# Making the low halves of six weight strips on GpSimd in a hybrid encoder block

## The chip, the cores and the metric

The kernel runs on one core of a Trainium2 chip. The metric is the device time of one execution in microseconds, the median over repeated runs. One execution was also profiled; every row below comes from that one.

## The reference

One encoder block on x of 512 tokens by 1024 channels, all in float32:

```
h = rms_norm(x);  z = h @ w_in                      # one combined projection
qa, ka, va, qb, kb, vb, ga, gb = split(z)
ya = axial_gqa_attention(qa, ka, va) @ w_o_a        # mixer A: 8 query heads on 2 key heads
yb = dilated_window_attention(qb, kb, vb) @ w_o_b   # mixer B: 12 heads in 3 dilation groups
x = x + (sigmoid(ga + ba) * ya + sigmoid(gb + bb) * yb) @ w_out
x = x + expert_choice_swiglu(rms_norm(x))           # 16 experts, 64 tokens each
y = rms_norm(x)
```

## The kernel before

Large matmuls are done in a rounded format on two parts of each operand, a high and a low half, and as three products (high by high, high by low, low by high). The weights of the projections come as *strips* of 128 columns: 128 partitions by 1024 float32, numbered in the order of use. A strip goes through four hands. SP loads it into a raw buffer (`w_raw`, a ring of four homes, L577 to L599; a load waits until the strip that had the home before is split). ScalarE copies it into `w_hi`, which rounds it (`split_hi`, L794 to L805, semaphore `w_hi_done`). VectorE subtracts, `w_lo = w_raw - w_hi` (`split_lo`, L1888 to L1892, semaphore `w_split`). TensorE waits for `w_split` before its first matmul with the strip (`wait_split`, L540).

Strips 0 to 11 make mixer A's q, k, v and mixer B's v. Strips 12 to 17 are the first q and k strips of mixer B, strips 18 and 19 the first two of its second half. All four engines have an order written out by hand.

Mixer A works on 32 tiles u (8 heads by 4 query tiles of 128). For each tile TensorE makes the scores (`scores_a`, L1326, two tiles ahead), VectorE takes the row maximum from PSUM (L2015), ScalarE the exponentials with their sum (L889), VectorE the reciprocal (L1985) and the product with it, the normalisation (L1987, `probs_normed`), TensorE turns the tile by transposes (`turn_probs`, L1357), ScalarE copies it out of PSUM (L901), and after each eight tiles TensorE multiplies by the values (`values_a`, L1369). Between the scores and the transposes of a tile TensorE does one to three steps of mixer B's q and k projection (`fill`, `col_steps`, L1169 to L1171). These steps read strips 12 to 18; the results are split too (L920 and L2003 for q, L923, L924, L2007 and L2008 for k).

VectorE's loop over the tiles places the low halves of strips 14 to 19 by the list `A_LOWS`:

```
if u in A_LOWS:                       # A_LOWS = (5, 7, 10, 16, 20, 26)
    split_lo(14 + A_LOWS.index(u))
```

Behind the loop VectorE waits for the distance table, copies a part of it (L2033) and goes on to mixer B, whose tiles it serves with L2052, L2058 and again L1985 and L1987. The later low halves (strip 20 on) stay with VectorE.

GpSimd has short work: the reciprocal square roots of the norms (`power`, L716 to L719, a TENSOR_SCALAR and a TENSOR_TENSOR with a power), the last ones for mixer A in the stretch from 50 to 63 us, then nothing until the second norm at 378 us, where it also makes three 128x512 subtractions (L755).

Of the kernel before, what the change touches and what calls it, by code (L numbers as in the profile page):

```python
# [84 lines left out]
def encoder_block(nc, x, norm1_g, w_in, b_gates, q_norm_g, k_norm_g, w_o_a, w_o_b, w_out, norm2_g,  # L85
# [139 lines left out]
    with ExitStack() as ctx:  # L225
# [250 lines left out]
        A_LEAD = 6  # L476
        A_FILL = [min(N_COL_A * KC, A_LEAD + 2 + (i + 1) * (N_COL_A * KC - A_LEAD - 2) // (NA - 1)) for i in range(NA)]
        O_READ, O_LOW = (10, 19, 26), (11, 21, NA)
        A_LOWS = (5, 7, 10, 16, 20, 26)
        B_HIGHS, B_LOWS = (NA + 4, NA + 6, NA + 7), (NA + 6, NA + 7, NA + 8)  # L480
        B_FILL = ([2, 3, 4, 5, 7, 8, 8, 8], [3, 6, 7, 8, 11, 14, 16, 16])

# [219 lines left out]
        @block.gpsimd  # L702
        def _(pool):
            pool.memset(neg_half, -0.5).then_inc(neg_half_set, 1)
            pool.memset(aff_wide[:, :, NE:2 * NE], 0.0).then_inc(masks_set, 1)
            pool.wait_ge(neg_half_set, 1)

            steps = [0]

            def settle(ins):  # L710

                ins.then_inc(pool_step, 1)
                steps[0] += 1
                pool.wait_ge(pool_step, steps[0])

            def power(sums, into, n, width, done):  # L716

                settle(pool.tensor_scalar(into, sums, 1.0 / width, EPS, ALU.mult, ALU.add))
                pool.tensor_tensor(into, into, neg_half[:, 0:n], ALU.pow).then_inc(done, 1)  # L719

            def power_of_sum(c):

                pool.wait_ge(ssq3, c + 1)
                settle(pool.tensor_scalar(rstd[:, c:c + 1], ssq[:, c:c + 1], 1.0, EPS, ALU.mult, ALU.add))
                pool.tensor_tensor(rstd[:, c:c + 1], rstd[:, c:c + 1], neg_half[:, 0:1], ALU.pow).then_inc(rstd3, 1)

            def rstd_of_x(c):
                pool.wait_ge(sumsq_done, c + 1)
                power(ssq[:, c:c + 1], rstd[:, c:c + 1], 1, D, rstd_done)

            for c in range(NT):
                rstd_of_x(c)

            w = A_HEADS + A_KV
            for c in range(NT):
                pool.wait_ge(a_sumsq, c + 1)
                power(ssqA[:, w * c:w * c + w], rstdA[:, w * c:w * c + w], w, HD, a_rstd)

            for c in range(NT):
                pool.wait_ge(sumsq2, c + 1)  # L740
                if c == NT - 1:
                    pool.wait_ge(sumsq2, NT + 1)
                    settle(pool.tensor_tensor(ssq[:, c:c + 1], ssq[:, c:c + 1], ssq_half[:, 0:1], ALU.add))
                power(ssq[:, c:c + 1], rstd[:, c:c + 1], 1, D, rstd2)
            pool.wait_ge(logits_done, NT)
            pool.memset(all_rows[:, :].bitcast(F32), 1.0).then_inc(masks_set, 1)
            pool.memset(later[:, 0:1].bitcast(F32), 0.0).then_inc(masks_set, 1)
            pool.memset(same_row[:, :, :, 0], 0.0).then_inc(masks_set, 1)
            pool.memset(same_row[:, :, :, 1:NT], 1.0).then_inc(masks_set, 1)
            pool.iota(row_steps[:, :], [[1, NT]], base=0, channel_multiplier=NT).then_inc(masks_set, 1)  # L750
            pool.wait_ge(aff_done, NT)
            for n, (c, h) in enumerate(LOW_BY_POOL):
                pool.wait_ge(xn_hi_done, c + 1)
                cols = slice(SEQ * h, SEQ * h + SEQ)
                pool.tensor_tensor(xn_lo[:, c, cols].rearrange("p (k i) -> p k i", k=HALF),  # L755
                                   x2[:, c, cols].rearrange("p (i k) -> p k i", k=HALF),
                                   xn_hi[:, c, cols].rearrange("p (k i) -> p k i", k=HALF).bitcast(F32),
                                   ALU.subtract).then_inc(xn_lo_pool, 1)
            pool.wait_ge(aff_lo_done, 1)
            pool.memset(ones_row[0:1, :], 1.0).then_inc(ones_row_set, 1)  # L760
            for c in range(NT):
                power_of_sum(c)
            pool.wait_ge(row_ms, 1)
            pool.tensor_tensor(ssq_half[:, 2:3], ssq_half[:, 2:3], neg_half[:, 0:1], ALU.pow).then_inc(rstd3, 1)
            pool.wait_ge(out_written, 16)
            pool.wait_ge(give_done, PAIRS)
            pool.wait_ge(fin_act_done, 1)
            pool.wait_ge(fin_done, NT + 1)
            pool.indirect_dma_start(out[0], bass.IndirectOffsetOnAxis(row_at[:, 0:1], 0), rows[:, :], None,
                                    bounds_check=SEQ - 1, oob_is_err=False).then_inc(rows_written, 16)  # L770
# [1089 lines left out]
        def _(dve):  # L1860
# [27 lines left out]
            def split_lo(n):  # L1888

                dve.wait_ge(w_hi_done, n + 1)  # L1890
                raw, hi, lo = parts_of(n)
                dve.tensor_tensor(lo, raw, hi.bitcast(F32), ALU.subtract).then_inc(w_split, 1)  # L1892
# [119 lines left out]
            for u in range(NA + 5):  # L2012
                if u < NA:
                    dve.wait_ge(score_done, u + 1)
                    dve.tensor_reduce(column(nmax, u), pp[u % 3][:, :], AX, ALU.max, negate=True)\  # L2015
                        .then_inc(nmax_done, 1)
                if 1 <= u <= NA:
                    norm_probs(u - 1, SEQ)
                for g in range(N_COL_A):
                    filled = filled_at(A_FILL, g)  # L2020
                    if u == (filled + 3 if g < N_COL_A - 1 else NA + 2):
                        low_col(g, 0)
                    if u == (filled + (6 if g == N_COL_A - 3 else 4) if g < N_COL_A - 1 else NA + 3):
                        low_col(g, 1)
                if u == 2:
                    low_k(1)
                if u in A_LOWS:
                    split_lo(14 + A_LOWS.index(u))
                if u in O_LOW:
                    low_o(O_LOW.index(u))  # L2030

            dve.wait_ge(dist_in, 16)
            settle(dve.tensor_copy(far[:, :], dist[:, 0, SEQ:SEQ + 2 * P]))  # L2033
            for hp in range(2):
                first, end = NA + 2 * NT * hp, NA + 2 * NT * (hp + 1)
                if hp:
                    for g in range(2 * NG + 2, 4 * NG):
                        low_col(g, 0)
                        low_col(g, 1)
                        split_lo(at[col_groups[g][1:]] + RING)  # L2040
                for u in range(first, end + 2):
                    if u == first + 1:
                        if hp == 0:
                            norm_probs(first, SEQ + 2 * P)
                        low_o(OA - 1 + hp)
                    if u < end:
                        head, c = divmod(u - NA, NT)

                        dve.wait_ge(score_done, NA + 2 * (u - NA) + 1)
                        dve.tensor_tensor(dist[:, c, SEQ:SEQ + 2 * P],  # L2052
                                          far_two[u % 2][:, 1, :, :].rearrange("p g n -> p (g n)"), far[:, :],
                                          ALU.add).then_inc(far_added, 1)
                        dve.wait_ge(far_added, u - NA + 1)
                        dve.wait_ge(score_done, NA + 2 * (u - NA) + 2)
                        wait_probs_free(dve, u)
                        dve.tensor_tensor_reduce(probs_of(u)[:, :], scores_two[u % 2], dist[:, c, :],  # L2058
                                                 -SLOPES[head], HUGE, ALU.add, ALU.min,
                                                 column(nmax, u)).then_inc(nmax_done, 1)  # L2060
                    if first + 1 - hp < u <= end:
                        norm_probs(u - 1, SEQ + 2 * P)
                    if hp == 0:
                        filled = first + filled_at(B_FILL[0], 0)
                        if u == filled + 3:
                            low_col(N_COL_A, 0)
                            low_col(N_COL_A, 1)
                        if u in B_LOWS:
                            split_lo(at[col_groups[2 * KC // RING + B_LOWS.index(u)][1:]] + RING)
                        if u == filled + 4:  # L2070
                            split_lo(at[col_groups[N_COL_A][1:]] + RING)
                    for g in range(2) if hp else ():
                        if u == first + filled_at(B_FILL[1], g) + 2:
                            split_lo(at[("ga", 0)] + g + RING)
# [378 lines left out]
```

## Time and profile before

| what | value |
|---|---|
| time, median of 3 runs | 862.43 us (862.28 to 864.42) |
| the profiled execution | 861.86 us |
| its span, first to last instruction | 859.8 us |
| granted TensorE clock, mean | 0.998 |
| TensorE busy | 839.4 us, 98% |
| VectorE busy | 379.3 us, 44% |
| ScalarE busy | 264.1 us, 31% |
| GpSimd busy | 29.0 us, 3% |
| HBM read | 235.92 MB |

Busy shares are means over stages with different limits; mixer A is the stretch from about 87 to 162 us, mixer B from there to about 245 us, the gates and the output projection to about 390 us, and the experts the rest. PE is TensorE's matmul side, PEld its weight loads, DVE is VectorE, ACT ScalarE, POOL GpSimd. In timelines the first number is the start and the second the duration, both in us.

### The profile page before, as it was taken

The page shows a single profiled execution, that of the slowest core. Times are in us where ns is not written, and L with a number is a line of the kernel's source. Part 1 is how long each engine was busy: PE and PEld are TensorE (multiplying, and loading weights), DVE is VectorE, ACT ScalarE, POOL GpSimd, SP SyncE. Part 2 cuts the span into 40 slices and gives each one's busy share as a digit, 9 for nine tenths or more (in the row PEclk, how much of TensorE's full clock was granted, in tenths as well). Part 3 has the DMA queues.
Part 4 walks back from the last instruction along what each step waited for, and adds up shares of the span by engine and source line. Part 5 has one row for each costly group of instructions (what it writes and reads, how often), then busy time and mean ns, then how long its engine had stood idle before and what let it go on. Part 6 is the DMA issues. An engine that isn't in the chain of part 4 may idle for free.

```text
span 859.8 us, 10399 instructions
## 1 busy us (share of the span) xinstructions
PE 839.4 (98%) x4197; PEld 513.2 (60%) x4197; DVE 379.3 (44%) x665; ACT 264.1 (31%) x461; POOL 29.0 (3%) x50
## 2 busy tenths in 40 slices
PE   9999999999999999999999999999999998989996
PEld 8898866687878888888534343344433433334343
DVE  6377987797715254427322237223131321321351
ACT  6333876695624233216011010010100101001231
POOL 1050000000000000003000000000000000000010
PEclk9999999999999999999999999999999999999999
DMA  9830112023034234884899999999999999999996
GB/s 285 179 98 2 50 50 98 25 76 109 20 123 143 84 107 144 311 356 180 331 410 425 429 428 426 429 428 427 428 428 427 426 430 428 426 423 429 427 420 265
DMA packets 81490, 239.19 MB, mean 278 GB/s; under 512 B 8102, under 2 KB 63526, under 8 KB 65828
## 3 DMA queue, kind: packets, MB, share of 16 engines
q1 hardware_dynamic: 76016, 235.94, 69.7%
q10 hardware_dynamic: 5284, 2.09, 1.0%
q8 instruction: 33, 0.54, 0.3%
q0 software_dynamic: 144, 0.51, 0.1%
q14 instruction: 13, 0.11, 0.0%
HBM read 235.92 MB, written 2.62 MB: 277 GB/s over the span
## 4 chain that ended last, share of the span: by engine, by line
PE 88%; DMA 8%; DVE 1%; ACT 1%; issue 1%; POOLq 0%; POOL 0%; SPq 0%; DVEq 0%; ACTq 0%
PE psum L1657 21%; PE psum L1169 11%; PE psum L1689 11%; PE psum L1171 11%; PE psum L1170 11%; DMA wslot<-in_w_down 7%; PE psum L1614 3%; PE psum L1708 3%; PE psum L1357 2%; PE psum L1818 2%; PE psum L1326 2%; PE psum L1369 1%; PE psum L1669 1%; PE psum L1175 1%; PE psum L1622 1%; PE psum L1379 1%
## 5 line engine op out<-in xcount | busy, mean ns | idle before, releaser
L1657 PE MATMUL psum<-wslot,xinT 128*64 128x512 f32 x1000 | 221.9, 595 | 3.7 <-DMA wslot<-in_w_up 1.9
L1657 PEld LDWEIGHTS psum<-wslot,xinT 128*64 128x64 f32 x1000 | 69.5, 137 | 141.3 <-issue 131.8
L1689 PE MATMUL psum<-wslot,actT 128*64 128x512 f32 x424 | 95.8, 596 | 4.5 <-DMA wslot<-in_w_down 4.5
L1169 PE MATMUL psum<-hT_hi,w_hi 128*128 128x512 f32 x208 | 82.4, 396 | 0.9 <-DVE oT_lo L1991 0.9
L1170 PE MATMUL psum<-hT_lo,w_hi 128*128 128x512 f32 x208 | 81.2, 390 | 0.0
L1171 PE MATMUL psum<-hT_hi,w_lo 128*128 128x512 f32 x208 | 81.2, 390 | 0.0
L1892 DVE TENSOR_TENSOR w_lo<-w_raw,w_hi 128x1024 fp32r<-128x1024 f32 (+1 forms) x46 | 52.9, 1174 | 44.4 <-ACT w_hi L805 44.3
L1689 PEld LDWEIGHTS psum<-wslot,actT 128*64 128x64 f32 x424 | 29.4, 137 | 60.4 <-issue 58.0
L1101 ACT ACTIVATE actT<-psum 128x512 f32<-128x512 f32 x16 | 9.6, 597 | 171.2 <-PE psum L1669 171.2
L2305 DVE TENSOR_TENSOR x<-x,psum 128x512 f32<-128x512 f32 x48 | 29.7, 681 | 57.0 <-PE psum L1708 57.0
L2295 DVE TENSOR_TENSOR y_lo<-psum,y_hi 64x512 fp32r<-64x512 f32 x28 | 19.3, 689 | 80.4 <-ACT y_hi L1111 80.0
L805 ACT ACTIVATE w_hi<-w_raw 128x1024 fp32r<-128x1024 f32 (+1 forms) x46 | 45.2, 1017 | 16.3 <-PE psum L1171 16.3
L1169 PEld LDWEIGHTS psum<-hT_hi,w_hi 128*128 128x128 f32 x208 | 39.0, 188 | 12.1 <-issue 2.8
L1171 PEld LDWEIGHTS psum<-hT_hi,w_lo 128*128 128x128 f32 x208 | 39.1, 188 | 8.4
L1170 PEld LDWEIGHTS psum<-hT_lo,w_hi 128*128 128x128 f32 x208 | 39.1, 188 | 7.8
L1096 ACT ACTIVATE act<-psum,slot_vals 128x512 f32<-128x512 f32 x16 | 11.0, 687 | 93.2 <-PE psum L1657 93.2
L2282 DVE SCALAR_TENSOR_TENSOR act<-psum,slot_vals,act 128x512 f32<-128x512 f32 x16 | 12.0, 750 | 59.1 <-ACT act L1096 59.0
L901 ACT ACTIVATE pT<-psum 128x512 f32<-128x512 f32 x48 | 28.5, 596 | 19.6 <-PE psum L1357 10.1
L1111 ACT ACTIVATE y_hi<-psum 64x512 fp32r<-64x512 f32 x28 | 16.5, 590 | 57.3 <-PE psum L1689 57.0
L1614 PE MATMUL psum<-xn,pick 128*128 128x512 f32 x120 | 29.4, 396 | 0.0
L2248 DVE TENSOR_TENSOR xinT<-psum,small 128x512 f32<-128x512 f32 x15 | 9.7, 686 | 40.0 <-PE psum L1622 40.0
L2288 DVE SCALAR_TENSOR_TENSOR act<-act,slot_fac,psum 128x512 f32<-128x512 f32 x16 | 12.0, 747 | 30.8 <-PE psum L1657 30.8
(285 smaller groups left out, 1306.5 us busy)
## 6 DMA issues: line engine op xcount, KB each, us to landing
wslot<-in_w_up SPq DMA_DIRECT2D x24, 2048.0 KB, 25.0
wslot<-in_w_gate SPq DMA_DIRECT2D x24, 2048.0 KB, 23.9
wslot<-in_w_down SPq DMA_DIRECT2D x22, 2048.0 KB, 22.4
w_raw<-in_w_in SPq DMA_DIRECT2D x34, 512.0 KB, 4.7
wslot<-in_w_up SPq DMA_DIRECT2D x15, 1024.0 KB, 11.0
wslot<-in_w_down SPq DMA_DIRECT2D x15, 1024.0 KB, 27.5
wslot<-in_w_gate SPq DMA_DIRECT2D x14, 1024.0 KB, 11.2
w_raw<-in_w_out SPq DMA_DIRECT2D x8, 512.0 KB, 4.9
```

The source lines that it names most:

```text
L805: act_.activation(hi, raw, ACT.Copy).then_inc(w_hi_done, 1)
L901: last = act_.activation(pT[:, head % 2, :, cols], tp[(0, 3)[u % 2]][:, :].rearrange("p (k i) -> p k i", i=P), ACT.Copy)
L1169: pe.matmul(out_, s_hi, m_hi, start=(k == 0), stop=False)
L1170: pe.matmul(out_, s_hi, m_lo, start=False, stop=False)
L1171: return pe.matmul(out_, s_lo, m_hi, start=False, stop=(k == n_k - 1))
L1614: mm = pe.matmul(bank[6 + f][:, :], pick[:, c, :, :], part[:, c, cols], start=(c == 0 and part is xn_hi), stop=(c == NT - 1 and part is xn ...
L1657: mm = pe.matmul(bank[2 * e + n][CAP * f:CAP * f + CAP, :], xinT[:, HALF * h + k, CAP * e:CAP * e + CAP], wslot[place_of(m)][:, k % PART, ...
L1689: mm = pe.matmul(bank[4 + e][CAP * f:CAP * f + CAP, :], actT[:, e, k, CAP * h:CAP * h + CAP], wslot[place_of(m)][:, k % PART, SEQ * f:SEQ ...
L1708: mm = pe.matmul(bank[added_bank(c, f)][:, :], give[:, p % 2, P * c:P * c + P], part[:, SEQ * f:SEQ * f + SEQ], start=(part is y_hi), stop ...
L1892: dve.tensor_tensor(lo, raw, hi.bitcast(F32), ALU.subtract).then_inc(w_split, 1)
L2295: dve.tensor_tensor(y_lo[rows, cols], bank[4 + e][CAP * f:CAP * f + CAP, :], y_hi[rows, cols].bitcast(F32), ALU.subtract).then_inc(y_lo_do ...
L2305: dve.tensor_tensor(part, part, bank[added_bank(c, f)][:, :], ALU.add).then_inc(added, 1)
```

## The change

The low halves of strips 14 to 19 are taken out of VectorE's loop and put into GpSimd's list, behind the reciprocal square roots of mixer A. GpSimd waits for the split before (`w_split` counts strips in order) and for the high half, and makes the same subtraction. VectorE waits, ahead of mixer B, until the last of the six is done, so that the count stays in order.

```
-        A_LOWS = (5, 7, 10, 16, 20, 26)
+        POOL_SPLITS = range(14, 20)
...
+            for n in POOL_SPLITS:
+                pool.wait_ge(w_split, n)
+                pool.wait_ge(w_hi_done, n + 1)
+                raw, hi, lo = parts_of(n)
+                pool.tensor_tensor(lo, raw, hi.bitcast(F32), ALU.subtract).then_inc(w_split, 1)
...
-                if u in A_LOWS:
-                    split_lo(14 + A_LOWS.index(u))
                 if u in O_LOW:
                     low_o(O_LOW.index(u))
 
             dve.wait_ge(dist_in, 16)
             settle(dve.tensor_copy(far[:, :], dist[:, 0, SEQ:SEQ + 2 * P]))
+            wait_split(dve, POOL_SPLITS[-1])
```

## Rows read from the trace of the kernel before

**Rows 1.** The page: busy time by engine; DMA share in 40 slices, in tenths.

```profile
PE 839.4 (98%) x4197; PEld 513.2 (60%) x4197; DVE 379.3 (44%) x665; ACT 264.1 (31%) x461; POOL 29.0 (3%) x50
...
DMA  9830112023034234884899999999999999999996
```

**Rows 2.** Windows: stretch, length, busy PE, PEld, DVE, ACT, POOL, clock, DMA share, GB/s.

```profile
75.00:100.00 25.00, 25.00 (x128) 20.62 (x127) 19.48 (x38) 17.02 (x33) 0.00 (x0) 1.00 0.00 1
...
120.00:140.00 20.00, 19.98 (x104) 14.05 (x103) 15.40 (x32) 14.06 (x30) 0.00 (x0) 1.00 0.18 51
...
405.00:860.00 455.00, 438.37 (x2068) 188.68 (x2066) 135.32 (x242) 59.39 (x98) 6.76 (x13) 1.00 0.98 414
```

**Rows 3.** Waits of TensorE's weight loads, 83 to 163 us: total, times, longest.

```profile
PEld psum L1357 <- DVE probs_a L1987: 2.1, 7, 0.5
```

**Rows 4.** Groups by form, VectorE: busy us, mean ns, idle before.

```profile
L1892 DVE TENSOR_TENSOR w_lo<-w_raw,w_hi 128x1024 fp32r<-128x1024 f32 x38 | 45.8, 1220 | 44.0 <-ACT w_hi L805 43.9
...
L1987 DVE TENSOR_SCALAR probs_a<-probs_a,small 128x512 f32<-128x512 f32 x32 | 15.6, 487 | 1.1
...
L1987 DVE TENSOR_SCALAR probs_b<-probs_b,small 128x768 f32<-128x768 f32 x16 | 9.9, 620 | 0.6
...
L1892 DVE TENSOR_TENSOR w_lo<-w_raw,w_hi 128x768 fp32r<-128x768 f32 x8 | 7.6, 952 | 0.4 <-ACT w_hi L805 0.4
```

**Rows 5.** Groups by form, the nearest subtractions and products of GpSimd and VectorE.

```profile
L755 POOL TENSOR_TENSOR xn<-x,xn 128x512 fp32r<-128x512 f32 x3 | 4.5, 1535 | 0.8 <-DVE aff_wide L2140 0.8
...
L718 POOL TENSOR_SCALAR small<-small 128x1 f32<-128x1 f32 x8 | 1.5, 192 | 338.2 <-ACT squares L1016 327.0 <-ACT squares L783 11.1
...
L2148 DVE TENSOR_TENSOR xn<-x,xn 128x512 fp32r<-128x512 f32 x5 | 5.4, 1092 | 1.9 <-ACT xn L1044 1.9
...
L1957 DVE TENSOR_TENSOR zA<-zA,small 128x640 f32<-128x640 f32 x4 | 3.3, 821 | 0.1
```

**Rows 6.** Timelines of GpSimd and VectorE, 50 to 62 us.

```profile
50.30 1.11 POOL L718 TENSOR_SCALAR small<-small 128x10 f32<-128x10 f32 x1 [34.95 <-DVE small L1951]
...
54.39 0.89 POOL L718 TENSOR_SCALAR small<-small 128x10 f32<-128x10 f32 x1
55.37 2.80 POOL L719 TENSOR_TENSOR small<-small 128x10 f32<-128x10 f32 x1
...
61.00 0.32 POOL L718 TENSOR_SCALAR small<-small 128x10 f32<-128x10 f32 x1
...
50.13 2.35 DVE L1892 TENSOR_TENSOR w_lo<-w_raw,w_hi 128x1024 fp32r<-128x1024 f32 x2
...
54.00 2.35 DVE L1892 TENSOR_TENSOR w_lo<-w_raw,w_hi 128x1024 fp32r<-128x1024 f32 x2
```

**Rows 7.** Timelines of ScalarE, VectorE and TensorE, 92 to 101 us.

```profile
92.69 1.05 ACT L805 ACTIVATE w_hi<-w_raw 128x1024 fp32r<-128x1024 f32 x1
...
93.86 0.49 DVE L1987 TENSOR_SCALAR probs_a<-probs_a,small 128x512 f32<-128x512 f32 x1
...
98.45 1.22 DVE L1892 TENSOR_TENSOR w_lo<-w_raw,w_hi 128x1024 fp32r<-128x1024 f32 x1
...
94.47 0.59 PEld L1357 LDWEIGHTS psum<-ident,probs_a 128*128 128x128 f32 x4
...
100.24 0.40 PE L1169 MATMUL psum<-hT_hi,w_hi 128*128 128x512 f32 x1
```

**Rows 8.** Timelines of the same engines, 119 to 125 us.

```profile
119.95 1.05 ACT L805 ACTIVATE w_hi<-w_raw 128x1024 fp32r<-128x1024 f32 x1
...
122.25 0.49 DVE L1987 TENSOR_SCALAR probs_a<-probs_a,small 128x512 f32<-128x512 f32 x1
...
124.02 0.59 PEld L1357 LDWEIGHTS psum<-ident,probs_a 128*128 128x128 f32 x4
```

**Rows 9.** Timelines of ScalarE and VectorE, 134 to 136 us.

```profile
134.22 1.06 ACT L805 ACTIVATE w_hi<-w_raw 128x1024 fp32r<-128x1024 f32 x1
...
135.43 0.49 DVE L1987 TENSOR_SCALAR probs_a<-probs_a,small 128x512 f32<-128x512 f32 x1
```

## The prediction

> **What bounds the kernel now.** I read the page first, then windows by stage, the waits, the groups of lines, and last the timelines of the instants at which the moved work runs. The page shows TensorE busy for 98% of the span, VectorE for 44%, GpSimd for 3%, and DMA near full only from the 21st slice of 40 on [rows 1]. The windows say which stage has which limit: from 75 to 162 us (mixer A) TensorE has no gap worth naming, at a granted clock of 1.00 (the 2.4 GHz level), while VectorE is busy over three quarters of the time and GpSimd does nothing; from 405 us the expert weights stream at 414 GB/s [rows 2]. TensorE's order is fixed, and the expert stream starts only when the stages before it have let go of SBUF, so a microsecond that TensorE loses in mixer A should reach the end of the kernel whole, and one gained too.
>
> VectorE is nearly a second bound there. The only VectorE wait that TensorE's weight loads show in mixer A is for normalised probabilities: 2.1 us in 7 waits, the longest 0.5 [rows 3]; the matmuls in flight cover it, for no matmul waits in that stretch. So 2.1 us is a ceiling on what a faster VectorE can return in this stage.
>
> **The change part by part.** *Removed from VectorE:* six subtractions of 1.22 us, 7.3 us in all [rows 4]. The trace has them at 98.45, 101.97, 108.47, 122.66, 135.83 and 148.51 us (the first stands in [rows 7]). Each sits right behind a normalisation and delays the next. Some of the seven waits come from this, others sit where no subtraction is; I take 0.3 us as the gain, between 0 and 2.1.
>
> *Added to GpSimd:* six subtractions 128x1024. The trace has none. The nearest row is its 128x512 subtraction, 1.535 us, which reads with a step; VectorE takes 1.092 us for that same stepped shape, yet 0.821 us for a plain 128x640 with two SBUF inputs [rows 5], which at 1.05 ns an element [rows 4] is 0.69 for a plain 512: a ratio of 1.6. Twice 1.535 less one fixed part of about 0.2 (a one-element GpSimd TENSOR_SCALAR takes 0.192 [rows 5]) gives 2.9 us as the upper end; dividing the per-element part, 2.7, by VectorE's 1.6 gives 1.9 as the lower end. I take 2.3, about the middle, since nothing says whether the step costs GpSimd as much as VectorE. The page GPSIMD Engine Reference (section 3) of the Trainium skill has 4.5 us for 2048 elements, which by halving would be an estimate of about 2.3 too.
>
> *When they run.* GpSimd now starts as soon as ScalarE has the high half, not where VectorE's list put it: the high halves, six rows of L805 of which the second, fifth and sixth stand in [rows 7, 8, 9], end at 91.17, 93.74, 98.02, 108.05, 121.00 and 135.28 us. With 2.3 us each, all low halves are ready earlier than now: the first by 94 us, where TensorE first reads that strip at 100.24 us and VectorE now finishes it only at 99.67 [rows 7]. Even 2.9 us each keeps 5 us of margin, and the later strips have more. So TensorE never waits for a strip. SP, which waits for a split before it refills that buffer, issues its loads of the next strips earlier; the DMA share of this stretch is 0.18 or less [rows 2], and ScalarE's place for the next high half is set by its list, so this costs and gives nothing. The new wait of VectorE on the sixth low half stands ahead of mixer B at 165.7 us, 25 us after GpSimd is done; behind it are the first scores of mixer B, but it costs at most a few hundredths. After 63.4 us GpSimd has nothing until 378 us, so nothing else queues behind the six.
>
> *The port.* This is where the change can hurt. GpSimd's four TENSOR_SCALARs of ten elements are the same work, yet took 1.11 us at 50.30, 0.89 at 54.39 and 0.32 at 61.00. The first ended at 51.41, just past the end at 51.35 of the VectorE subtraction started at 50.13; the second at 55.28, past the end at 55.22 of the one started at 54.00 [rows 6]. So GpSimd waits for a whole VectorE instruction with two SBUF inputs: something is exclusive between the two engines. What the trace doesn't show is the reverse, a long GpSimd read in front of VectorE. The VectorE instruction at risk in mixer A is the normalisation L1987: 0.487 us for 512 elements and 0.620 for 768, that is 0.52 ns an element where the subtraction with two inputs needs 1.05 (1.220 against 0.952 us for 1024 and 768) [rows 4]. It moves two elements at a time. The other VectorE instructions of the stage read PSUM and at most one SBUF tensor. I take it that what holds one way holds the other: a GpSimd subtraction reading 1024 elements of two tensors keeps L1987 out from its start to its end.
>
> The page SBUF — State Buffer (section "Who interferes with whom") of the Trainium skill says the shared pair is an exclusive lock, kept for the full instruction by whichever engine came first, with the other wholly blocked, and names tensor_scalar in its two-port mode among those that take it. By that rule the sum below holds; if only VectorE can hold GpSimd up, rival (a) does. The trace, 51.41 behind 51.35 us, agrees in one direction; no row of it has the other.
>
> *The cost, if GpSimd blocks the normalisation.* Due times are the L1987 starts, need times the L1357 loads of the same tile.
> Strips one to three: the first subtraction runs 91.46 to 93.76 (it waits for the normalisation that began at 90.97) and hits nothing. The second starts at about 93.82, just ahead of the normalisation due at 93.86 [rows 7], which then ends at 96.12 + 0.49 = 96.61 where TensorE wanted it at 94.47: 2.15 lost. The third falls, everything being shifted, beside the normalisation due at 98.05 or the next: between 0.45 and 2.3 more; I take 0.5.
> Strip four, at 108 us, lies under the attention values (normalisations are 3.8 us early there): 0.
> Strip five: 121.44 to 123.74; the normalisation due at 122.25 ends at 124.23, wanted at 124.02 [rows 8]: 0.2.
> Strip six: ready to start at 135.28 + 0.08, and the normalisation is due at 135.43 [rows 9]; if GpSimd is first it ends at 137.66 + 0.49 = 138.15 instead of 135.92: 2.2.
> Sum 2.15 + 0.5 + 0.2 + 2.2 = 5.1, less 0.3 gained: 4.8 us. Lost TensorE time isn't given back, because behind it TensorE is again the bound.
>
> The profiled execution took 861.86 us (span 859.8 and 2.1 around it), so it would come to 866.7; it stands 0.6 under the median of the runs, 862.43, and against that median the forecast is 867.2 us.
>
> **The rivals.** What this kernel's measurement can tell from no change is about 0.3%, 2.6 us.
> (a) *GpSimd doesn't hold VectorE up*, or does so piece by piece. For: the GpSimd power at 55.37, 2.80 us long, left VectorE's list without a gap [rows 6]; against: it reads ten elements. Then only the 0.3 gain and the wait remain: 862.1 to 862.9, the same. This is the outcome on the other side; it decides if L1987 stays at 0.49 us during GpSimd's subtractions.
> (b) *It blocks, but the near ties fall VectorE's way.* At 93.82 against 93.86 and 135.36 against 135.43 there are under 0.1 us between the two. If VectorE comes first both times, GpSimd starts 0.5 later and hits only the following normalisation: about 0.4 each. With 0.45 and 0.2 the sum is 1.5, less 0.3: 863.6, the same within what can be told.
> (c) *All ties fall GpSimd's way and an operation is 2.9 us:* 2.8 + 2.3 + 1.4 + 2.8 = 9.3, less 0.3: 871.4.
> (d) *VectorE's relief is worth more than the waits show.* To be faster by 2.6 us it would have to return more than the whole 2.1 of waits. A gain of that kind would need the relief to reach mixer B, where VectorE waits for ScalarE anyway: 859.5.
> (e) *GpSimd becomes late with a strip.* It needs an operation above 6 us, twice the upper bound; under 2%.
>
> **How the numbers follow.** Blocking with a loss above 2.6 us (the forecast, and (c) as its tail) 0.53; (b) 0.15; (a) 0.28; (d) 0.04. Slower by over 0.3%: 0.53; within: 0.43; faster: 0.04. The likeliest case alone spans 865.0 to 871.4. The range for 8 in 10 has to take in (a), so it goes from 861.9 to 870.3, and leaves out (d) and most of (c).
>
> **What would show it.** Six TENSOR_TENSOR rows on GpSimd between 91 and 138 us, of 1.9 to 2.9 us; L1987 with a few instances of 2 us or more, or late starts behind them, at the second and the sixth; the waits of L1357 for L1987 rising from 2.1 us to about 7; mixer B's first score matmul starting about 4.8 us later, and the distances unchanged from there. If L1987 keeps a maximum of 0.5 us, the port step is wrong and (a) holds. If GpSimd's rows are longer than 2.9 us because VectorE interrupts them, the lock isn't held for the whole instruction. If the loss sits behind 165 us instead, the added wait did it and my reading of the order is wrong.

## The result, and the profile after

| | before | after |
|---|---|---|
| median | 863.13 us | 868.59 us |
| lowest to highest, 10 runs each | 861.93 to 865.23 | 865.83 to 871.63 |
| ratio, 95% interval | | 1.0064 (1.0050 to 1.0079) |
| profiled execution | 861.86 us | 868.40 us |
| its span | 859.8 us | 866.6 us |
| granted TensorE clock, mean | 0.998 | 0.993 |

The change makes the kernel slower by 0.64%. The forecast was 867.2 us against 862.43, a ratio of 1.0055. Four executions of the experiments below took far longer than all others of their version (e1 once 1430.6 us, e2 955.6 and 4871.8, e4 955.77); they are counted in the medians given there, not in the ratios.

The page of the changed kernel, busy time by engine, answers to [rows 1]. Line numbers behind L743 are 4 to 6 higher than before: L1987 is now L1993, L1357 is L1363, L805 is L811.

```profile
PE 842.4 (97%) x4197; PEld 515.6 (60%) x4197; DVE 381.0 (44%) x659; ACT 264.4 (31%) x461; POOL 43.6 (5%) x56
```

GpSimd gained 14.6 us. VectorE lost six subtractions of 1.22 us, 7.3 us, and yet is busy 1.7 us longer, not shorter. The groups by form show where the time went; columns as in [rows 4]:

```profile
L743 POOL TENSOR_TENSOR w_lo<-w_raw,w_hi 128x1024 fp32r<-128x1024 f32 x6 | 14.6, 2440 | 62.1 <-ACT w_hi L811 62.1
...
L1898 DVE TENSOR_TENSOR w_lo<-w_raw,w_hi 128x1024 fp32r<-128x1024 f32 x32 | 38.5, 1220 | 44.0 <-ACT w_hi L811 43.9
L1993 DVE TENSOR_SCALAR probs_a<-probs_a,small 128x512 f32<-128x512 f32 x32 | 23.6, 738 | 1.1
```

The 32 normalisations of mixer A went from 487 ns on average [rows 4] to 738: 8.0 us more for the same work. (8.0 less 7.3 is 0.7 of VectorE's 1.7; the page counts time in which any instruction runs, the groups add up instructions, which overlap at their ends.) The timelines of GpSimd and VectorE (start, duration) show that few of them carry all of it:

```profile
94.07 2.36 POOL L743 TENSOR_TENSOR w_lo<-w_raw,w_hi 128x1024 fp32r<-128x1024 f32 x1 [0.15 <-ACT w_hi L811]
100.53 2.62 POOL L743 TENSOR_TENSOR w_lo<-w_raw,w_hi 128x1024 fp32r<-128x1024 f32 x1 [4.10 <-ACT w_hi L811]
109.94 2.36 POOL L743 TENSOR_TENSOR w_lo<-w_raw,w_hi 128x1024 fp32r<-128x1024 f32 x1 [6.80 <-ACT w_hi L811]
123.67 2.54 POOL L743 TENSOR_TENSOR w_lo<-w_raw,w_hi 128x1024 fp32r<-128x1024 f32 x1 [11.37 <-ACT w_hi L811]
137.95 2.35 POOL L743 TENSOR_TENSOR w_lo<-w_raw,w_hi 128x1024 fp32r<-128x1024 f32 x1 [11.75 <-ACT w_hi L811]
...
91.17 0.48 DVE L1993 TENSOR_SCALAR probs_a<-probs_a,small 128x512 f32<-128x512 f32 x1
...
94.05 2.66 DVE L1993 TENSOR_SCALAR probs_a<-probs_a,small 128x512 f32<-128x512 f32 x1
...
100.40 0.49 DVE L1993 TENSOR_SCALAR probs_a<-probs_a,small 128x512 f32<-128x512 f32 x1
...
101.59 1.83 DVE L1993 TENSOR_SCALAR probs_a<-probs_a,small 128x512 f32<-128x512 f32 x1
...
110.93 1.66 DVE L1993 TENSOR_SCALAR probs_a<-probs_a,small 128x512 f32<-128x512 f32 x1
...
123.47 0.49 DVE L1993 TENSOR_SCALAR probs_a<-probs_a,small 128x512 f32<-128x512 f32 x1
...
124.78 1.71 DVE L1993 TENSOR_SCALAR probs_a<-probs_a,small 128x512 f32<-128x512 f32 x1
...
137.96 2.63 DVE L1993 TENSOR_SCALAR probs_a<-probs_a,small 128x512 f32<-128x512 f32 x1
```

Add start and duration: the stretched normalisation of 94.05 ends at 96.71, where GpSimd's operation ends at 96.43; the others end 0.27 to 0.29 us behind theirs in the same way (103.42 and 103.15, 112.59 and 112.30, 126.49 and 126.21, 140.59 and 140.30). VectorE holds GpSimd up too: the two operations that began just behind the start of a normalisation (100.53 behind 100.40, 123.67 behind 123.47) took 2.62 and 2.54 us instead of 2.36.

What reached TensorE: the waits from 83 to 168 us (the weight loads' answer to [rows 3]; then the matmuls', of which before had none), and the two matmuls that waited.

```profile
PEld psum L1363 <- DVE probs_a L1993: 6.1, 5, 2.6
...
PE psum L1363 <- DVE probs_a L1993: 3.9, 2, 2.2
```
```profile
96.77 0.44 PE L1363 MATMUL psum<-ident,probs_a 128*128 128x128 f32 x2 [1.73 <-DVE probs_a L1993]
...
140.65 0.66 PE L1363 MATMUL psum<-ident,probs_a 128*128 128x128 f32 x4 [2.17 <-DVE probs_a L1993]
141.06 0.98 PE L1332 MATMUL psum<-kA,qA 128*128 128x512 f32 x2
141.83 0.63 PE L1175 MATMUL psum<-hT_hi,w_hi 128*128 128x512 f32 x1
...
143.97 0.63 PE L1177 MATMUL psum<-hT_hi,w_lo 128*128 128x512 f32 x1
...
145.46 0.39 PE L1175 MATMUL psum<-hT_hi,w_hi 128*128 128x512 f32 x1
```

Two gaps, each behind one of the two longest normalisations. Behind the second the projection matmuls take 0.63 us instead of 0.39 for some 3.4 us. The windows say why; the eighth column is the granted clock:

```profile
75.00:100.00 25.00, 23.27 (x118) 19.05 (x117) 19.54 (x34) 15.50 (x30) 4.77 (x2) 1.00 0.15 43
...
140.00:145.00 5.00, 4.36 (x17) 3.53 (x18) 3.50 (x8) 2.04 (x5) 0.31 (x1) 0.66 0.36 105
145.00:150.00 5.00, 5.00 (x28) 4.16 (x27) 4.22 (x9) 4.64 (x9) 0.00 (x0) 1.00 0.02 4
```

Full clock, 2.4 GHz, around the first gap and again from 145 us; a mean of 0.66 between 140 and 145, that is the 1.2 GHz level for about two thirds of it, after an idle stretch of 2.17 us. The start of each matmul, compared with the start of the same matmul before, gives the account: 0.2 us were there at 80 us already (the clock was low from 8 to 12 us too, a mean of 0.57 where before has 1.00), 1.9 come at the first gap, 0.3 and 0.2 at the next two tiles' transposes, 2.1 at the last gap, 1.5 in the slow stretch. Mixer B's first score matmul stands at 169.0 us (lines grouped by source; the last numbers are first and last start) where it stood at 162.8, and the last one at 234.6 against 228.4, 6.2 later both times.

```profile
L1344 PE MATMUL psum<-kB,qB x24: 278/282/384, 169.0 to 234.6; 128*128 128x256 f32 x24
```

Behind that nothing is given back: the matmuls are still 6.2 us late at 600 us, 0.6 more is lost in the last 260 us, where the experts run, and the profiled execution takes 6.5 us longer (its span 6.8).

### The profile page after: what moved, and what is told of

Same layout as the page of the kernel before. It is cut to its first block, busy times and chain, and to the rows that moved or that the text cites. A ratio compares the mean times of both kernels' runs of the same rounds, so it can differ in the third digit from the quotient of the medians.

```text
span 866.6 us, 10405 instructions
## 1 busy us (share of the span) xinstructions
PE 842.4 (97%) x4197; PEld 515.6 (60%) x4197; DVE 381.0 (44%) x659; ACT 264.4 (31%) x461; POOL 43.6 (5%) x56
## 3 DMA queue, kind: packets, MB, share of 16 engines
HBM read 235.92 MB, written 2.62 MB: 275 GB/s over the span
## 4 chain that ended last, share of the span: by engine, by line
PE 86%; DMA 8%; DVE 3%; ACT 1%; issue 1%; POOLq 0%; POOL 0%; SPq 0%; DVEq 0%; ACTq 0%
PE psum L1663 21%; PE psum L1695 11%; PE psum L1175 11%; PE psum L1176 11%; PE psum L1177 11%; DMA wslot<-in_w_down 7%; PE psum L1620 3%; PE psum L1714 3%; PE psum L1363 2%; PE psum L1824 2%; PE psum L1332 1%; PE psum L1375 1%; PE psum L1675 1%; PE psum L1181 1%; PE psum L1628 1%; DVE probs_a L1993 1%
## 5 line engine op out<-in xcount | busy, mean ns | idle before, releaser
L1898 DVE TENSOR_TENSOR w_lo<-w_raw,w_hi 128x1024 fp32r<-128x1024 f32 (+1 forms) x40 | 45.6, 1166 | 44.4 <-ACT w_hi L811 44.3
L811 ACT ACTIVATE w_hi<-w_raw 128x1024 fp32r<-128x1024 f32 (+1 forms) x46 | 45.2, 1017 | 16.3 <-PE psum L1177 16.3
L2021 DVE TENSOR_REDUCE small<-psum 128x1 f32<-128x512 f32 x32 | 21.9, 687 | 9.4 <-PE psum L1332 9.0
```

Of the source, the lines that this page charges most:

```text
L811: act_.activation(hi, raw, ACT.Copy).then_inc(w_hi_done, 1)
```

## The experiments

The theory: a GpSimd operation keeps the normalisation out from its start to its end, and each operation costs what the normalisation due then is late for TensorE. The rivals: the added wait or the new order costs it elsewhere; GpSimd and VectorE only slow each other down, whatever their accesses; the whole kernel's timing moved for another reason. "Shift" is how much later than before mixer B's first score matmul starts (before: 162.8 us); it measures mixer A alone. The median takes in whatever else varies: the runs of before alone go from 861.37 to 865.48 us over the experiments.

### One part of the change alone

**e1_free**: only strips 14 and 17 on GpSimd, whose operations were forecast to hit nothing; the rest back in VectorE's loop.

```
-        POOL_SPLITS = range(14, 20)
+        POOL_SPLITS = (14, 17)
+        A_LOWS = {7: 15, 10: 16, 20: 18, 26: 19}
...
+                if u in A_LOWS:
+                    dve.wait_ge(w_split, A_LOWS[u])
+                    split_lo(A_LOWS[u])
```

> Only strips 14 and 17 are made by GpSimd, the two whose subtraction met no normalisation in the changed kernel; VectorE keeps 15, 16, 18 and 19 at their old places. Port theory: no normalisation is stretched on TensorE's path, so the time is that of before, ratio 0.999 to 1.001. If it is instead GpSimd's work as such, or the wait on the other engine's count, that costs, a third of the loss of the change shows, about 1.002.

Measured: 864.9 us median against 862.45, ratio 1.0014 (1.0000 to 1.0029), lowest 861.89; profiled execution 862.16, shift −0.1. No matmul waits. One normalisation is stretched all the same:

```profile
109.33 2.01 DVE L1994 TENSOR_SCALAR probs_a<-probs_a,small 128x512 f32<-128x512 f32 x1
```

It lies under the attention values, where the normalisations are ahead of TensorE. So blocking as such costs nothing; it costs where the blocked tile is due. This rests on the profiled execution. The ratio lies between what was expected (0.999 to 1.001) and what the rival asked (1.002) and doesn't decide, and the profile gives no reason for the median's 2.4 us: its own time is that of before.

**e2_first_two**: strips 14 and 15 on GpSimd (`POOL_SPLITS = (14, 15)`, `A_LOWS = {10: 16, 16: 17, 20: 18, 26: 19}`).

> Strips 14 and 15 are made by GpSimd, 16 to 19 by VectorE. Port theory: the second GpSimd subtraction, from about 94.1 us, stretches one normalisation to about 2.6 us and TensorE loses 2.1 us once: 2.0 us more than before (ratio 1.002 to 1.003), and up to 1.8 us more on top if the granted clock falls for a while behind the gap. Nothing else changes. The rival that the loss grows with the number of GpSimd subtractions gives the same as with the two free strips.

Measured: 864.87 against 862.45, ratio 1.0024 (1.0013 to 1.0034), shift 2.1.

```profile
93.83 2.37 POOL L744 TENSOR_TENSOR w_lo<-w_raw,w_hi 128x1024 fp32r<-128x1024 f32 x1 [0.17 <-ACT w_hi L812]
...
93.80 2.68 DVE L1994 TENSOR_SCALAR probs_a<-probs_a,small 128x512 f32<-128x512 f32 x1
...
96.53 0.66 PE L1364 MATMUL psum<-ident,probs_a 128*128 128x128 f32 x4 [1.74 <-DVE probs_a L1994]
```

The first gap of the full change, made by strip 15 alone.

**e3_last_alone**: strip 19 alone (`POOL_SPLITS = (19,)`, `A_LOWS = {5: 14, 7: 15, 10: 16, 16: 17, 18: 18}`).

> Only strip 19 is made by GpSimd; VectorE makes strip 18 two tiles earlier, so that GpSimd can start right at the high half, as in the changed kernel. Port theory: the tie with the normalisation of tile 19 decides. If GpSimd starts first or at once with it, one normalisation of about 2.6 us and 2.2 us lost, ratio about 1.0025, plus 1.7 us if the clock falls behind it; if VectorE is first, 0.4 us or less and ratio 1.000.

Measured: 866.14 against 862.45, ratio 1.0036 (1.0024 to 1.0048), shift 3.8, the dearest of the six. The gap is 2.17 us, and behind it the clock falls as it did in the full change:

```profile
138.30 1.12 PE L1364 MATMUL psum<-ident,probs_a 128*128 128x128 f32 x4 [2.17 <-DVE probs_a L1994]
```
```profile
138.00:142.00 4.00, 3.70 (x12) 3.13 (x13) 3.25 (x8) 2.05 (x5) 0.00 (x0) 0.57 0.47 131
```

Matmul by matmul, 0.2 us of the shift were there before, 2.1 come at the gap and 1.5 in the slow stretch. The two parts cost 2.1 + 2.1 without the clock, nearly all that the full change costs without it (4.4, below). The cost adds up by operation; the other four add little.

### The same work at other instants

**e4_vector_first**: all six on GpSimd, but strips 15 and 19 wait until the normalisation that they tie with is done. This forces rival (b).

```
+        POOL_AFTER = {15: 2, 19: 19}
...
                 pool.wait_ge(w_hi_done, n + 1)
+                if n in POOL_AFTER:
+                    pool.wait_ge(probs_normed, POOL_AFTER[n] + 1)
```

> All six on GpSimd as in the change, but GpSimd lets the normalisation of tile 2 (before strip 15) and of tile 19 (before strip 19) go first, so VectorE wins the two ties. Port theory: those two normalisations take 0.49 us again and the following ones are held up for part of an operation; of the 4.3 us lost, some 1.3 to 2.5 remain, ratio 1.0015 to 1.003. If the lock were not held for the whole instruction, or if the loss were GpSimd's lateness, delaying its start could only cost: ratio at or above the changed kernel's 1.006.

Measured: 865.72 against 862.45, ratio 1.0038 (1.0023 to 1.0053), shift 2.7, no clock drop; the ratio expected was 1.0015 to 1.003. The two ties are gone, but the third operation now starts in front of a normalisation that is due at once:

```profile
98.16 2.36 POOL L746 TENSOR_TENSOR w_lo<-w_raw,w_hi 128x1024 fp32r<-128x1024 f32 x1 [1.25 <-ACT w_hi L814]
...
98.88 1.93 DVE L1996 TENSOR_SCALAR probs_a<-probs_a,small 128x512 f32<-128x512 f32 x1
...
100.86 0.66 PE L1366 MATMUL psum<-ident,probs_a 128*128 128x128 f32 x4 [1.80 <-DVE probs_a L1996]
```

A wait in the right place for one operation moves the next collision: 2.0 of the 2.7 us come at this one, and of the 4.4 us that the collisions of the full change cost (e10, below) 2.7 remain.

**e5_under_values**: the same code with `POOL_AFTER = {15: 8, 16: 9, 17: 16, 18: 17, 19: 24}`: each operation starts with the stretch of attention values, when VectorE is ahead.

> All six on GpSimd, but each from the second on is let go only behind a normalisation after which the attention values give VectorE slack (behind tiles 8, 9, 16, 17 and 24). Port theory: every stretched normalisation lies under the 3.6 us of the values, TensorE waits for L1987 no longer than before (2.1 us in its weight loads, none in its matmuls), and the time is that of before or up to 1 us less: ratio 0.998 to 1.001. Rival, that work on GpSimd costs as such or comes too late for its strip: ratio above 1.003.

Measured: 861.7 against 862.4, ratio 0.9992 (0.9981 to 1.0003), shift 0.0. All six stand on GpSimd and the added wait ahead of mixer B is there. The waits of the weight loads, and the most stretched normalisation beside the load that reads its tile, 1.3 us after its end:

```profile
PEld psum L1366 <- DVE probs_a L1996: 1.1, 3, 0.5
```
```profile
109.03 2.10 DVE L1996 TENSOR_SCALAR probs_a<-probs_a,small 128x512 f32<-128x512 f32 x1
...
112.43 0.59 PEld L1366 LDWEIGHTS psum<-ident,probs_a 128*128 128x128 f32 x4
```

**e11_placed_again**: the same kernel once more, on the chip of e10.

> The version with the subtractions under the attention values once more: ratio 0.998 to 1.0005 to before.

Measured: 861.82 against 862.3, ratio 0.9990 (0.9978 to 1.0002). Both are the same as before within what can be told. The relief of VectorE shows, 1.0 us less of waits than [rows 3], and buys nothing that these runs can tell from noise, since matmuls in flight covered those waits anyway. It is the fastest version tried, and not measurably faster than the kernel before.

### What is held, and by what access

**e6_write_only**: GpSimd sets the low halves to zero and reads nothing. The products with these six low halves are thereby left out in value, not in time.

```
-                pool.tensor_tensor(lo, raw, hi.bitcast(F32), ALU.subtract).then_inc(w_split, 1)
+                pool.memset(lo.bitcast(F32), 0.0).then_inc(w_split, 1)
```

> As the change, but GpSimd fills the six low halves with zeros instead of subtracting (so the products with these low halves are left out): it writes SBUF and reads none, at the same places. From its 128x128 memset (0.20 us) and 128x40 (0.13) some 0.95 us for 1024 elements. If the normalisation needs GpSimd's write port too, the one beside the second fill is stretched to at most 1.4 us and TensorE loses under 1 us; if only the read port is shared, all L1987 stay at 0.49 us. Time in both cases within 1 us of before.

Measured: 864.44 against 862.3, ratio 1.0019 (1.0008 to 1.0030), shift 2.2.

```profile
93.90 0.95 POOL L743 MEMSET w_lo<- 128x1024 f32 x1 [1.51 <-ACT w_hi L811]
98.92 0.95 POOL L743 MEMSET w_lo<- 128x1024 f32 x1 [4.07 <-ACT w_hi L811]
...
93.91 1.23 DVE L1993 TENSOR_SCALAR probs_a<-probs_a,small 128x512 f32<-128x512 f32 x1
...
98.83 1.33 DVE L1993 TENSOR_SCALAR probs_a<-probs_a,small 128x512 f32<-128x512 f32 x1
```

94.85 and 95.14, 99.87 and 100.16: the normalisation again ends 0.29 us behind GpSimd. The expectations that TensorE would lose under 1 us and that the time would stay within 1 us of before (it came 2.1 above) failed: the memset starts beside three due normalisations and each costs 0.3 to 0.9 us of matmul time, 2.0 in all. So writing alone is enough to hold the normalisation up. Whether reading alone is too wasn't tried. The page SBUF — State Buffer of the Trainium skill (section "Who interferes with whom") has the shared read and write ports as one pair, taken whole by the two-port form of tensor_scalar; that fits.

**e7_halves**: each subtraction as two of 512 elements.

```
-                pool.tensor_tensor(lo, raw, hi.bitcast(F32), ALU.subtract).then_inc(w_split, 1)
+                for k in (0, HALF):
+                    some = slice(k, k + HALF)
+                    last = pool.tensor_tensor(lo[:, some], raw[:, some], hi[:, some].bitcast(F32), ALU.subtract)
+                last.then_inc(w_split, 1)
```

> As the change, but each GpSimd subtraction is two of 512 elements, about 1.3 us each, nothing between them. Port theory with the lock held for one instruction: VectorE gets in between the two, the longest normalisation falls from 2.66 to some 1.5 us, and of the 4.3 us lost about half remains, ratio 1.002 to 1.004. If GpSimd keeps the port over both, the normalisations stay at 2.6 us and the ratio at 1.006.

Measured: 864.58 against 862.4, ratio 1.0018 (1.0007 to 1.0029). The profiled execution (867.54) was 2.7 us late ahead of mixer A already; less that, the shift is 2.2. The ratio expected was 1.002 to 1.004. The longest normalisation is the one in the last place, beside the first half of the last subtraction:

```profile
139.27 1.28 POOL L745 TENSOR_TENSOR w_lo<-w_raw,w_hi 128x512 fp32r<-128x512 f32 x1 [11.41 <-ACT w_hi L814]
...
139.28 1.55 DVE L1996 TENSOR_SCALAR probs_a<-probs_a,small 128x512 f32<-128x512 f32 x1
```

It ends at 140.83, 0.28 us behind this half's end at 140.55: VectorE gets in between the halves. What is held is held for one instruction, and halving it halved the loss, 2.2 us against 4.4. One more pair is of use below: here VectorE's normalisation got through and GpSimd's half was the longer one.

```profile
96.60 0.49 DVE L1996 TENSOR_SCALAR probs_a<-probs_a,small 128x512 f32<-128x512 f32 x1
...
96.69 1.55 POOL L745 TENSOR_TENSOR w_lo<-w_raw,w_hi 128x512 fp32r<-128x512 f32 x1
```

**e8_one_port**: the change, with mixer A's normalisation in a form that also writes a sum.

```
-                dve.tensor_scalar(p, p, column(rinv, u), None, ALU.mult).then_inc(probs_normed, 1)
+                if u < NA:
+                    dve.tensor_scalar(p, p, column(rinv, u), 0.0, ALU.mult, ALU.add,
+                                      accum_out=small[:, 200 + u % 4:201 + u % 4]).then_inc(probs_normed, 1)
+                else:
+                    dve.tensor_scalar(p, p, column(rinv, u), None, ALU.mult).then_inc(probs_normed, 1)
```

> As the change, but mixer A's normalisation also writes a sum that nobody reads, which should keep it at one element a step (0.69 us and a short read of the sum instead of 0.49). Port theory: it then has one SBUF tensor and one port, and no instance is longer than 0.75 us although GpSimd's subtractions run beside it; the kernel is slower than before by what 32 longer normalisations cost, and equals the companion run without GpSimd within 1 us. Rival, that GpSimd holds up any VectorE instruction on SBUF: instances of over 2 us remain, and this run is 4 us or more above its companion.

**e9_one_port_before**: the same form in the kernel before, to compare e8 with.

> The companion: the kernel before with the same one-element normalisation in mixer A. All theories: instances of about 0.69 us plus a read of about 0.1, VectorE 9 to 10 us busier in mixer A, TensorE waiting for it more often, 3 to 8 us slower than before.

Measured: e8 864.45 (shift 2.4), e9 866.06 (shift 4.3), both against 862.4; ratios 1.0023 (1.0012 to 1.0034) and 1.0039 (1.0024 to 1.0053). The sources of the two, minimum, median and maximum in ns, e8 first:

```profile
L1994 DVE TENSOR_SCALAR_CACHE_REDUCE probs_a<-probs_a,small x32: 745/746/749, 89.8 to 164.0; 128x512 f32<-128x512 f32 x32
```
```profile
L1988 DVE TENSOR_SCALAR_CACHE_REDUCE probs_a<-probs_a,small x32: 745/746/747, 89.9 to 165.9; 128x512 f32<-128x512 f32 x32
```

This form takes 746 ns whether GpSimd works beside it or not. In e8 GpSimd makes all six subtractions, in 2.37 to 2.41 us, and no normalisation is stretched. Here the move to GpSimd gains: e8 is 1.6 us below e9 by the medians and 1.9 by the shift, more than the 1 us apart that was expected: where each normalisation is slower, VectorE's relief is worth something, with 7.1 us of weight loads' waits in e9 and 4.3 in e8. That settles it: the change hurts only through what the normalisation in its fast form (487 ns) shares with GpSimd. As a cure it is no use, since the slower form costs more (4.3 us of shift) than the move brings.

### The change again

**e10_change_again**: the changed kernel once more.

> The changed kernel once more, on one chip with the placed version. Port theory: two normalisations of about 2.6 us, ratio 1.004 to 1.008 to before; whether the granted clock falls behind the second gap varies from run to run or not, and is worth 1.7 us.

Measured: 868.07 against 862.3, ratio 1.0059 (1.0039 to 1.0078), lowest 866.37, which is also the profiled one. It has the same two gaps, 1.7 and 2.17 us, and the same waits (3.9 in two), but behind the second gap the clock stays up:

```profile
138.00:145.00 7.00, 4.83 (x26) 3.85 (x25) 6.38 (x11) 4.69 (x12) 2.10 (x1) 1.00 0.26 76
```
```profile
140.44 0.66 PE L1363 MATMUL psum<-ident,probs_a 128*128 128x128 f32 x4 [2.17 <-DVE probs_a L1993]
140.85 0.70 PE L1332 MATMUL psum<-kA,qA 128*128 128x512 f32 x2
141.39 0.39 PE L1175 MATMUL psum<-hT_hi,w_hi 128*128 128x512 f32 x1
```

The shift is 4.4 us here: that is the cost of the collisions alone; the slow stretch, where it comes, adds 1.5.

## Why the prediction was right

The mechanism and the side were right, and the sum, 4.8 us, stands beside 4.4 without the fall of the clock and 6.0 with it (6.2 less the 0.2 that were there before).

- *GpSimd's operation*: 2.3 us taken, 2.35 to 2.41 measured, and up to 2.62 behind a normalisation. The 2.3 was the middle taken between bounds of 1.9 and 2.9; no row of before gave it, so that it was met this closely is in part luck. The starts were forecast to within 0.3 us up to the second; later ones moved with the shift.
- *The lock, from start to end*: shown for the subtraction by rows in both directions, for one instruction at a time by e7, and as the cause by e8 and e9.
- *Strip 2 (number 15)*: 2.15 forecast; 1.9 at the gap and 0.3 at the next tile, because VectorE's whole list was late. e2 has it alone: 2.1.
- *Who comes first*: the two dear ties were forecast GpSimd's way, with 0.04 and 0.07 us between the two. The recorded starts came nearer still, 94.07 against VectorE's 94.05 and 137.95 against 137.96, the first the other way round, and GpSimd held VectorE up all the same. It did so in every profile with these ties (the change and e10 both, e2 and e3 one each), so it is no accident of one execution; but no row of before said so, and that the forecast took this side is in part luck.
- *Strip 3*: 0.5 forecast, "between 0.45 and 2.3 more". The normalisation was stretched by 1.34 us, but the weight loads waited 0.46 and the matmuls lost 0.2. A normalisation that comes first, at 100.40, had kept GpSimd back and its successor was not yet due.
- *Strip 4*: 0 forecast, 0 measured. *Strip 5*: 0.2 forecast; the normalisation at 124.78 took 1.71 and nobody waited, since the one at 123.47 had come before GpSimd and was the one that was due.
- *Strip 6*: 2.2 forecast, 2.1 measured, in e3 2.1.
- *The gain of 0.3*: none is seen. The waits that vanished were covered by matmuls in flight, as the ceiling of 2.1 us allowed.
- *The added wait and the order*: e5 has both at no cost.
- *A reading that was off*: the DMA share of the stretch was called 0.18 or less; that holds from 120 to 140 us, while from 100 to 120 it is 0.27. Nothing in the sum hung on it.
- *Missing from the sum*: the granted clock. TensorE's forecast gap of 2.2 us was counted as 2.2 us; in the profiled execution and in e3 the clock was at its lower level for some 3.4 us behind it, 1.5 more.
- *The median*: it came 1.4 above the forecast. Of this 0.7 is the median of before, 863.13 over ten runs and not 862.43. The rest isn't taken apart: three of the change's ten runs stand at 865.8 to 866.0 us (mean clock 0.997), three at 867.9 to 868.8 (0.993, the profiled one among them) and four at 870.7 to 871.6 (0.995 to 0.997). The clock can stand behind the step from the first group to the second, not behind the third. That the median fell this near to the forecast is in part luck.

Rival (b), ties for VectorE, was priced at 1.5 less 0.3; forced in e4 it cost 2.7. Its sum priced each operation against the timeline of before, and the third one moved into a worse place once the first tie was turned. Rival (a) is refuted, (c) asked for operations of 2.9 us and for ties that went the other way at the third and fifth, (d) and (e) didn't happen.

What stays open: the runs of before lie in two groups, about 862 and about 864.6 us, without a cause that these profiles show, and the medians of e1 and e2 take part in it; those of the change go up to 871.6, more than the clock's 1.5 explains. Some profiles (e2, e4, e7) lose another microsecond in the expert stage. Why the clock falls behind the same 2.17 us gap in one execution and not in the other is not settled either.

## What to carry to other kernels

Before work is moved from VectorE to an idle GpSimd, look for VectorE instructions in a form like this case's tensor_scalar at 0.52 ns an element and lay the GpSimd operations over the timeline: one that starts ahead of such an instruction, or within some hundredths of a microsecond of its recorded start, keeps it until it ends itself. Put the operations where the engine behind VectorE has slack, tied to VectorE's progress, and cut long ones, since the hold lasts one instruction. If VectorE's waits are covered anyway, as here, even the best placement may bring nothing that can be measured (0.9992 and 0.9990 here, both intervals reaching 1), and the simple version is to be kept.

## What the runs showed of the hardware

- The recorded start of a VectorE instruction doesn't say who was first. Against a subtraction, at 94.05 and 94.07 and in e2 at 93.80 and 93.83, VectorE stands in front by 0.02 to 0.03 us and was blocked; at 96.60 and 96.69 (e7) and at 100.40 and 100.53 it stands 0.09 and 0.13 in front and got through. Against the memset of e6 it was blocked even 0.09 in front, at 98.83 and 98.92, and 0.10 in front, at 108.63 and 108.73. So a lead in the record below 0.13 us leaves it open.
- A blocked normalisation ends 0.27 to 0.29 us behind GpSimd's instruction, less than its own 0.49: part of it seems to be under way, or its start to be counted, while it waits.
- A GpSimd memset of 1024 elements (0.95 us), which reads nothing, holds the normalisation too.
- The same kernel with the same gap of 2.17 us had the clock halved for some 3.4 us in one execution (0.66 over 140 to 145 us) and not in another (1.00 over 138 to 145 us). Behind the gaps of 1.73 to 1.80 us (the change, e10, e2, e4) the clock stayed up each time.
